# A two-part transformer program on one core: the order of the tiles within an SBUF partition

## The reference

```
h = rms_norm(x, norm_mix_w);  z = h @ w_in + b_in            # 1024 x 5640
ya = dilated_mixture_attention(rope(aq), rope(ak), av)       # 8 heads of 64
yb = sigmoid(mo) * norm(mlstm_chunkwise(silu(conv(mq, mk)), mv, mi, mf))
mixed = sigmoid(ga) * (ya @ w_proj_att) + sigmoid(gb) * (yb @ w_proj_mlstm)
x = x + mixed @ w_out
x = x + square(relu(rms_norm(x, norm_mlp_w) @ w_ff1)) @ w_ff2   # 1024 x 4096 and back
...
xn = _rmsnorm(h, norm1_w);  proj = xn @ w_in                 # second part
merged = g0 * (y_ssd @ w_up_ssd) + g1 * (y_att @ w_up_attn) + g2 * (y_pool @ w_up_pool)
h = h + merged @ w_out
h = h + (silu(a_part) * b_part) @ w_ffn_out                  # 1024 x 2*2816 and back
```

## Time and profile before

| what | us |
|---|---|
| median of 3 runs (2549.46 to 2552.08) | 2551.91 |
| the profiled execution: its own time | 2553.61 |
| its span, first to last instruction | 2551.8 |
| TensorE busy with matmuls (11732) | 2482.3 |
| TensorE weight loads, beside the matmuls | 1995.6 |
| GpSimd busy | 1096.6 |
| VectorE busy | 996.0 |
| ScalarE busy | 869.9 |

### The profile page before, as it was taken

How to read it: one execution, slowest core, us unless ns; L and a number is a source line. 1 busy time by engine, 2 the same in 40 slices (tenths; PEclk the granted TensorE clock), 3 DMA queues, 4 the chain that set the end, 5 groups by cost and what they waited for, 6 DMA issues and landing times.

```text
span 2551.8 us, 30042 instructions
## 1 busy us (share of the span) xinstructions
PE 2482.3 (97%) x11732; PEld 1995.6 (78%) x11732; DVE 996.0 (39%) x1582; ACT 869.9 (34%) x1093; POOL 1096.6 (43%) x808
## 2 busy tenths in 40 slices
PE   8899999999999999899999999999999999999998
PEld 6767788888888867688888888798776678888887
DVE  4545564310212354565320212557585544322202
ACT  4245333331323345333431223442224323322213
POOL 3332344554544422435554554442343244455542
PEclk9999999999999999999999999999999999999999
DMA  4221223222322221223222222231122123223221
GB/s 137 83 67 50 66 83 99 87 96 98 99 99 84 86 67 50 74 75 99 83 99 99 92 92 81 83 92 50 52 89 65 59 95 99 91 91 97 99 99 66
DMA packets 174028, 215.18 MB, mean 84 GB/s; under 512 B 7652, under 2 KB 155044, under 8 KB 173924
## 3 DMA queue, kind: packets, MB, share of 16 engines
q1 hardware_dynamic: 171572, 210.39, 25.5%
q10 hardware_dynamic: 2352, 3.31, 0.4%
HBM read 211.20 MB, written 2.10 MB: 84 GB/s over the span
## 4 chain that ended last, share of the span: by engine, by line
issue 50%; POOL 30%; PE 19%; DMA 0%; POOLq 0%; DVE 0%; ACT 0%; SPq 0%
POOL w_lo L289 30%; PE ps L328 3%; PE ps L329 3%; PE ps L330 3%; PE ps L735 3%; PE ps L1752 2%; PE ps L1754 2%; PE ps L1756 2%; DMA w_raw<-in_w_in 0%; POOLq L300 0%; PE ps L317 0%; PE ps L321 0%; PE ps L318 0%; PE ps L348 0%; PE ps L354 0%
## 5 line engine op out<-in xcount | busy, mean ns | idle before, releaser
L289 POOL TENSOR_TENSOR w_lo<-w_raw,w_hi 128x512 fp32r<-128x512 f32 x804 | 1096.4, 1395 | 1428.2 <-ACT w_hi L275 1416.3
L275 ACT ACTIVATE w_hi<-w_raw 128x2048 fp32r<-128x2048 f32 x200 | 383.0, 1915 | 1054.8 <-PE ps L330 395.9
L735 PE MATMUL ps<-h_hi,w_hi 128*128 128x512 f32 (+1 forms) x936 | 396.7, 424 | 13.9 <-POOL w_lo L289 13.8
L735 PE MATMUL ps<-h_hi,w_lo 128*128 128x512 f32 (+1 forms) x936 | 370.3, 396 | 0.0
L735 PE MATMUL ps<-h_lo,w_hi 128*128 128x512 f32 (+1 forms) x936 | 370.2, 396 | 0.0
L328 PE MATMUL ps<-h_hi,w_hi 128*128 128x512 f32 x816 | 319.1, 391 | 0.0
L330 PE MATMUL ps<-h_hi,w_lo 128*128 128x512 f32 x816 | 317.6, 389 | 0.0
L329 PE MATMUL ps<-h_lo,w_hi 128*128 128x512 f32 x816 | 317.5, 389 | 0.0
L735 PEld LDWEIGHTS ps<-h_hi,w_hi 128*128 128x128 f32 (+1 forms) x936 | 176.6, 189 | 75.9 <-issue 21.1
L735 PEld LDWEIGHTS ps<-h_lo,w_hi 128*128 128x128 f32 (+1 forms) x936 | 176.9, 189 | 43.6 <-issue 7.8
L735 PEld LDWEIGHTS ps<-h_hi,w_lo 128*128 128x128 f32 (+1 forms) x936 | 176.4, 188 | 42.0
(11 more groups left out here) (408 smaller groups left out, 3677.2 us busy)
## 6 DMA issues: line engine op xcount, KB each, us to landing
w_raw<-in_w_in SPq DMA_DIRECT2D x72, 1024.0 KB, 5.1
w_raw<-in_w_ff SPq DMA_DIRECT2D x64, 1024.0 KB, 5.2
w_raw<-in_w_ffn_in SPq DMA_DIRECT2D x22, 1024.0 KB, 5.0
w_raw<-in_w_out SPq DMA_DIRECT2D x12, 1024.0 KB, 5.1
w_raw<-in_w_ffn_out SPq DMA_DIRECT2D x11, 1024.0 KB, 4.9
w_raw<-in_w_proj_att SPq DMA_DIRECT2D x4, 1024.0 KB, 5.0
w_raw<-in_w_proj_mlstm SPq DMA_DIRECT2D x4, 1024.0 KB, 5.0
w_raw<-in_w_up_ssd SPq DMA_DIRECT2D x4, 1024.0 KB, 5.0
```

The source lines that it names most:

```text
L275: act.activation(k.whi[:, slot * SLOT:(slot + 1) * SLOT], k.wraw[:, slot * SLOT:(slot + 1) * SLOT], ACT.Copy).then_inc(k.hi_done, CHUNKS)
L289: pool.tensor_tensor(k.wlo[:, a:a + T], k.wraw[:, a:a + T], k.whi[:, a:a + T], ALU.subtract)\
L735: mm = pe.matmul(out, lhs, rhs, start=i == 0 and n == 0, stop=stop and n == 2)
```

## The change

Only the places of tiles in a partition change. No instruction is added, removed or moved; the instructions of all engines stand in the same order in both programs.

```diff
+ARENA = 25728
...
         k = Kern(nc, ctx)
+        k.hhi, k.hlo = k.keep("h_hi", KD * T, F32R), k.keep("h_lo", KD * T, F32R)
+        k.whi, k.wlo = k.keep("w_hi", 2 * SLOT, F32R), k.keep("w_lo", 2 * SLOT, F32R)
+        k.arena, k.arena_words = (k.top + 127) // 128 * 128, ARENA
+        k.top = k.arena + 4 * ARENA
         k.xT = k.keep("xT", KD * T)
-        k.hhi, k.hlo = k.keep("h_hi", KD * T, F32R), k.keep("h_lo", KD * T, F32R)
         k.wraw = k.keep("w_raw", 2 * SLOT)
-        k.whi, k.wlo = k.keep("w_hi", 2 * SLOT, F32R), k.keep("w_lo", 2 * SLOT, F32R)
         k.cst = k.keep("constants", C_END)
...
-        k.arena = (k.top + 127) // 128 * 128
-        k.arena_words = (nc.sbuf_usable_end() - k.arena) // 4 if callable(nc.sbuf_usable_end) else (nc.sbuf_usable_end - k.arena) // 4
```

## The result

| | before | changed |
|---|---|---|
| median, us | 2550.68 (4 runs, 2549.31 to 2552.08) | 2531.02 (4 runs, 2527.44 to 2531.77) |
| profiled execution, own time, us | 2553.61 | 2531.77 |
| its span, us | 2551.8 | 2529.9 |
| TensorE busy, us | 2482.3 | 2459.5 |

The ratio of the changed kernel to the one before is 0.992, with a 95% interval of 0.9903 to 0.9937. The median fell by 19.7 us; 6.4 were forecast.

A forecast was written before the change was run, and what follows sets the result against it. TensorE's start-to-start distances were taken as the bound. Gains of 3.4 (`ff`), 0.85 (`s_ff`), 0.5 (`s_mixed`), 0.1 (`mixed`), 1.3 (`yb`) and 0.2 us (`s_ya`), taken as 6.4, gave 2545.5 us; range 2535 to 2554.

The forecast's parts named there:

- Bound and engines: Whole kernel: TensorE 97% busy, its start-to-start distances set the time; moving `xT` and `w_raw` taken as 0.
- no sign that the stationary place matters: Weights moved from 82048 up to 49280 up: cost and gain 0 for the matmuls on h.
- The count: Matmuls reading the arena's halves: 3408 at 6.67 ns each, 22.7 us, worked out under rival 2.
- rival 2: Whole arena becomes fast because the start's remainder modulo 256 counts, not height: 22.7 us, 2529; chance 0.13.
- What differs is where the moving tile lies: Up against Down: moving tiles below 65664 take 226.7 ns, those at or above 126208 take 233.3.
- That is a step and no slope: Arena tiles from 126208 to 224768: the same 6.7 ns extra per 512-column matmul wherever they lie.
- a step above 114816: Moving weights at 82048 to 114816, 120 ns for 256 columns, read as fast; step put between 114816 and 126208.
- A distance is long if its matmul or the one before it is far.: Down's triples with only the middle tile high in the partition: two of three long, 231.1 ns average, gain 6.67 ns per triple.
- Rival 1: Each matmul on a high-lying tile pays only for itself: 11.9 to 12.4 us gained, about 2540; chance 0.22.
- Rival 3: Step at or below 82048, so the arena stays slow: no change, within 3 us of 2551.9; chance 0.21.
- rival 4: Switching between low and high moving tiles within a triple holds the long value: slower, 2562; chance 0.11.
- The rule of the Trainium skill: TensorE never waits on anyone and no rule concerns place within a partition: the change would be worth 0.

The follow-up runs named there:

- experiment 9: Changed kernel with weight halves, arena and what lies above moved up 128 bytes, h left in place: 2552.95 us, ratio 1.001 to the kernel before.
- experiment 1: Kernel before with the arena alone moved up 128 bytes: 2530.81 us, ratio 0.9925.
- experiment 2: Changed kernel with its arena and what lies above it moved up 128 bytes: 2549.27 us, ratio 0.9998 to the kernel before.
- experiment 3: Changed kernel with every tile 128 bytes higher: 2527.93 us, ratio 0.9912; run once more, 2529.86 us.
- experiment 8: Matmuls alone, no reference computation, in other types and widths: float32 429 ns, bfloat16 216 ns at every difference; fp32r varies at 256 and 384 columns.
- experiment 5: Matmuls alone with finer start steps and alternating tiles: 228.4 ns where the own weight tile matches, 230.0 where the next one does.
- experiment 4: Matmuls alone, no reference computation, at chosen starts of moving and weight tiles: 226.7 ns at d = 0, 228.9 for mixed triples.
- experiment 6: Kernel before with `ff_lo` and the two scratch tiles behind it moved 128 bytes, in the first part: 2543.63 us, ratio 0.9976.

## Why the prediction was right in sign and wrong in size

**Bound and engines.** Right. TensorE's distances are the time, and moving `xT` and `w_raw` cost nothing that shows in it. Up kept 226.7 ns, as said. The stationary tile's height is worth nothing, but its start is: experiment 9 moves the weights against h, and the distances change. The prediction's "no sign that the stationary place matters" rested on rows with d = 0 alone.

**The count.** Right. 3408 matmuls, and 6.67 ns each: 22.7 us worked out for rival 2, 21.2 measured on the sums.

**"What differs is where the moving tile lies" and "That is a step and no slope".** This is the step that failed. Height and remainder went together in the kernel before: everything low was at 128 above a multiple of 256, everything in the arena at a multiple. I chose height, so I left `ff_lo`, `s_ff_lo`, `mixed_hi`, `s_mixed_lo`, `ya`, `ys` and `s_yp` slow and gave Down half a gain. Measured, all 3408 matmuls are fast after the change, 21.2 us and not 6.4. Experiments 1 and 2 separate the two causes: moving the arena by 128 bytes gives the whole gain without the new order, and takes it away with it; remainder has all of it and height none.

That the time fell at all, as forecast, is therefore luck: by the cause that was forecast nothing would have changed, and the new order happened to end on matching remainders. The rows did not carry "no slope" as well as I wrote: the 405 ns of `ys_hi` stands beside no idle time, so no wait explains it.

The evidence brought against the remainder was the job with 8-column weight tiles, whose period "doesn't follow them". That was misread: those rows begin at the job's second triple. The first is the only one whose weight tile begins at d = 0, and the timeline of the kernel before has it as

```profile
67.80 0.39 PE L735 MATMUL ps<-h_hi,w_hi 128*8 128x512 f32 x1
...
68.48 0.40 PE L735 MATMUL ps<-h_hi,w_hi 128*8 128x512 f32 x1
```

0.68 us, 226.3 ns each, and each of the seven behind it takes 0.69, 231 ns; so it is in both layers. In experiment 9, where d is 0 at the fifth weight tile and no longer at the first, the fifth triple of the second layer is the one with 0.68 (the first layer shows none). So the trace of before held a sign for the remainder, one triple ahead of the rows that were taken against it.

The evidence for a step above 114816 was the moving weights. They have d = 0, and at 256 columns the matmuls alone take 120.0 there, about the worst, and 113.3 at best: the 32 cycles over the columns that looked like "near" were a coincidence. These rows had only one value in the trace, and nothing to compare it with.

**"A distance is long if its matmul or the one before it is far."** Wrong, in the kernel and alone. Slow, fast, slow has a mean of 228.9, not 233.3, and fast, slow, fast 228.9, not 231.1. The entrance and exit of Down gave one excess more than there are matmuls, and many rules fit a single such number. It had no part in the result here, since no mixed triple is left.

**Rival 2** had the number, 22.7 us, and was given 0.13. Its condition was half right: a multiple of 256 is not slow by itself (experiment 3, 2527.93 us with every tile at one), only a difference from the weight tile's remainder is.

**Rival 1** had the right mean for fast, slow, fast and the wrong premise. **Rival 3**'s step and **rival 4**'s loss by switching didn't occur: the mixed stretches are below 233.3.

**The rule of the Trainium skill.** The page "SBUF — State Buffer", section "Who interferes with whom", by which TensorE never waits, would have had 0. The trace and the runs disagree by up to 6.7 ns per matmul of 512 fp32r columns. "Back-to-back issue gap" of the Trainium skill's page "TensorE: Matmul & The Clock Gate" has 215.8 ns for 512 columns, from a formula that it gives for the gap of an isolated matmul; for a stream of them it has about 131. In the streams here the 215.8 agrees to the digit with the bfloat16 row of experiment 8, and with no fp32r row, and no run shows 131.

**What stays open.** Why the difference matters. The slow start of each run in experiment 9 and the change of the best difference with the width suggest that the reads of the moving tile and of some weight tile disturb each other, but the alternating stretches of experiment 5 fit neither "own" nor "next", and I know of no rule that gives the table there. A version with the units of moving weights shifted by 192 bytes, worth up to 1152 times 6.7 ns, 7.7 us, by the 256-column stretches, was not tried.

## What to carry to other kernels

When one shape has two distances in one trace, list everything in which the two groups of operands differ, the starts modulo 256 among it, and shift one tile by 128 bytes before any larger reordering is credited. In fp32r kernels with 512-column matmuls and 128-column weights start the moving and the weight tiles at the same remainder of 256 bytes; that cost one line here (experiment 1) and gave 0.75%. For 256 columns it is the wrong rule by the matmuls alone (experiments 5 and 8). A row without a counterpart that differs in one thing only is no evidence for or against a theory.

## What had not been expected of the hardware

- With d the start of the moving tile less that of the weight tile, modulo 256 bytes: fp32r at 512 columns takes 226.7 ns at d = 0, 228.9 at 64, and 232.4 to 234.3 at the other multiples of 32; among differences that are no multiple of 32 the worst is 240.0. Float32 (429) and bfloat16 (215.8) don't care.
- The best difference depends on the width: at 256 columns 113.3 ns for 192 and 120.0 for 0; at 128 columns 111.6 to 111.7 throughout.
- A mixture of slow and fast tiles is not the mean of its parts: one slow in three costs 2.2 ns per matmul, which is its share, but two in three cost 2.2 as well, and three in three 6.7 (experiments 4 and 6).
- A faster TensorE changed which of two other engines waits. The product `merged` times `gate` on VectorE, in the kernel before and then in the changed one (groups by line: count, busy us, mean ns, idle before):

```profile
L1425 DVE TENSOR_TENSOR merged<-merged,gate 128x512 f32<-128x512 f32 x16 | 19.4, 1213 | 0.5
```

```profile
L1426 DVE TENSOR_TENSOR merged<-merged,gate 128x512 f32<-128x512 f32 x16 | 15.2, 952 | 0.6
```

It looks like one more effect of the places, since it is 953 ns with the arena of the kernel before 128 bytes up and 1217 with the changed kernel's arena alone up. But the mean mixes two kinds, and the timelines of one such instruction, before and then changed, show another cause:

```profile
371.59 1.29 POOL L289 TENSOR_TENSOR w_lo<-w_raw,w_hi 128x512 fp32r<-128x512 f32 x1
371.62 1.81 DVE L1425 TENSOR_TENSOR merged<-merged,gate 128x512 f32<-128x512 f32 x1
```

```profile
371.48 0.70 DVE L1426 TENSOR_TENSOR merged<-merged,gate 128x512 f32<-128x512 f32 x1
371.60 1.73 POOL L290 TENSOR_TENSOR w_lo<-w_raw,w_hi 128x512 fp32r<-128x512 f32 x1
```

Before, GpSimd starts its `w_lo` 0.03 us ahead of VectorE and takes 1.29 us, and VectorE takes 1.81 and not 0.70. With the change TensorE delivers 0.14 us earlier, VectorE starts 0.12 us ahead of GpSimd, and it is GpSimd that takes 1.73. The one that starts second takes longer; in the same instruction and its three repetitions in all eleven traces of whole kernels, 18 to 68 ns of a lead for GpSimd go with 1.76 to 1.82 us on VectorE, and 57 to 126 ns of a lead for VectorE with 0.69 to 0.71 on VectorE. So it is the order of the starts, which TensorE's speed shifts. These 4.2 us of VectorE were hidden behind TensorE, and so was what GpSimd paid for them.
